# Token tile as the outer loop of the output projection and router, a slot list made on chip, and a gated down bias in one fp32r product

## What is computed

```python
h = h + memory_cross_attention(rmsnorm(h, norm_xa_g), mem, ...)   # ends in: o @ xa_wo
xt = rmsnorm(h, norm_ffn_g).reshape(n, d)
logits = xt @ router_w + router_b
top_val, top_idx = lax.top_k(logits, 4)
gates = softmax(top_val)
# tokens sorted by expert; slot_tok[slot] = token of that slot
gu = xt[tok] @ w_gu[e] + b_gu[e]
g, u = minimum(gu[:, :F], 7.0), clip(gu[:, F:], -7.0, 7.0)
y = ((u + 1.0) * (g * sigmoid(1.702 * g))) @ w_down[e] + b_down[e]
h = h + scatter_add(y * gates)
```

## Time and profile before

| | |
|---|---|
| median of 3 runs | 2607.06 us (2603.6 to 2607.36) |
| the profiled execution | 2609.65 us, of which the span from first to last instruction is 2608.0 us |
| PE busy | 2352.2 us (90%) |
| DVE busy | 1590.6 us (61%) |
| ACT busy | 1117.3 us (43%) |
| POOL busy | 350.5 us (13%) |
| mean granted clock of PE | 0.93 of full speed |

### The profile page before, as it was taken

How to read it: one execution, slowest core, us unless ns; L and a number is a source line. 1 busy time by engine, 2 the same in 40 slices (tenths; PEclk the granted TensorE clock), 3 DMA queues, 4 the chain that set the end, 5 groups by cost and what they waited for, 6 DMA issues and landing times.

```text
span 2608.0 us, 31503 instructions
## 1 busy us (share of the span) xinstructions
PE 2352.2 (90%) x9494; PEld 1711.6 (66%) x9495; DVE 1590.6 (61%) x1522; ACT 1117.3 (43%) x1047; POOL 350.5 (13%) x338
## 2 busy tenths in 40 slices
PE   7997499989999956999999999999999999999960
PEld 4553374554554525888888888888888787778840
DVE  4446841110131366786876666787778779978748
ACT  4123120030130213565654544556566567765632
POOL 0370300000000052010110100111011011110016
PEclk9989659989999957999999999999999999999985
DMA  4002010130100116786876866778789789997857
GB/s 151 33 1 83 1 81 33 35 126 29 36 19 1 67 66 235 289 302 222 327 268 225 290 224 211 281 278 324 254 313 369 247 313 370 371 338 267 313 209 289
DMA packets 215265, 514.21 MB, mean 197 GB/s; under 512 B 19140, under 2 KB 19338, under 8 KB 214520
## 3 DMA queue, kind: packets, MB, share of 16 engines
q1 hardware_dynamic: 194912, 450.72, 48.5%
q0 software_dynamic: 18352, 62.60, 6.4%
q10 hardware_dynamic: 1960, 0.35, 0.1%
HBM read 481.97 MB, written 30.48 MB: 196 GB/s over the span
## 4 chain that ended last, share of the span: by engine, by line
PE 44%; issue 5%; DVE 5%; DMA 5%; ACT 2%; POOL 1%; DVEq 1%; ACTq 0%; POOLq 0%; SPq 0%
PE PS L839 17%; PE PS L860 10%; PE PS L843 9%; PE PS L867 5%; DVE WL L1602 2%; DMA WA<-in_exp_w_down 2%; DMA WA<-in_exp_w_gu 2%; PE PS L892 1%; PE PS L831 1%; DVE H L1212 1%; PE PS L804 1%; POOL WA L1884 1%; ACT WH L1112 1%; ACT WH L1117 1%; DVE XEL L1598 0%
## 5 line engine op out<-in xcount | busy, mean ns | idle before, releaser
L1602 DVE TENSOR_TENSOR WL<-WA,WH 128x2048 fp32r<-128x2048 f32 x384 | 876.6, 2290 | 288.4 <-ACT WH L1133 117.8
L839 PE MATMUL PS<-WH,XEL 128*128 128x512 f32 x1344 | 361.1, 391 | 0.0
L839 PE MATMUL PS<-WH,XEH 128*128 128x512 f32 x1344 | 360.7, 390 | 0.0
L843 PE MATMUL PS<-WL,XEH 128*128 128x512 f32 x1344 | 347.6, 390 | 0.0
L1117 ACT CAST WH<-WA 128x2048 fp32r<-128x2048 f32 x128 | 243.9, 1908 | 201.8 <-PE PS L843 150.5
L1112 ACT CAST WH<-WA 128x2048 fp32r<-128x2048 f32 x128 | 244.5, 1910 | 190.4 <-PE PS L843 155.0
L1133 ACT CAST WH<-WA 128x2048 fp32r<-128x2048 f32 x124 | 236.5, 1909 | 199.3 <-PE PS L867 181.8
L839 PEld LDWEIGHTS PS<-WH,XEL 128*128 128x128 f32 x1344 | 253.2, 188 | 53.3
L843 PEld LDWEIGHTS PS<-WL,XEH 128*128 128x128 f32 x1344 | 253.2, 188 | 52.9
L839 PEld LDWEIGHTS PS<-WH,XEH 128*128 128x128 f32 x1344 | 253.1, 188 | 52.1
L538 PE MATMUL PS<-XT,WB 128*128 128x512 f32 x512 | 223.2, 597 | 1.1 <-issue 1.1
(11 more groups left out here) (249 smaller groups left out, 2373.4 us busy)
## 6 DMA issues: line engine op xcount, KB each, us to landing
WA<-in_exp_w_gu SPq DMA_DIRECT2D x256, 1024.0 KB, 6.4
WA<-in_exp_w_down SPq DMA_DIRECT2D x128, 1024.0 KB, 6.1
y_rows<-WA POOLq DMA_DIRECT2D x42, 512.0 KB, 6.7
WB<-in_xa_wkv SPq DMA_DIRECT2D x4, 2048.0 KB, 8.0
WB<-in_w_in SPq DMA_DIRECT2D x3, 2048.0 KB, 10.4
H<-in_x SPq DMA_DIRECT2D x4, 1024.0 KB, 5.9
WB<-in_w_out SPq DMA_DIRECT2D x2, 2048.0 KB, 7.8
WA<-in_x SPq DMA_DIRECT2D x1, 4096.0 KB, 12.2
```

The source lines that it names most:

```text
L839: nc.tensor.matmul(PS[:, 2 * h + t, :], x[:, KT4 * half + k, t * P:(t + 1) * P], WH[:, j % 4, k * HALF:(k + 1) * HALF], start=False, stop= ...
L843: ins = nc.tensor.matmul(PS[:, 2 * h + t, :], XEH[:, KT4 * half + k, t * P:(t + 1) * P], WL[:, j % 4, k * HALF:(k + 1) * HALF], start=Fals ...
L1602: v.tensor_tensor(WL[:, s, :], RAW[:, s, :], WH[:, s, :].bitcast(F32), sub).then_inc(done, 1)
```

## The change

It has four pieces.

- **Tile outermost.** The units are ordered per tile: both halves of `wo2`, then `xt3` of the tile before, `rl` of the one before that and `rt` of the one before that. DVE makes the one-hot, `MS` and `CU` of each tile as its top 8 come in. The up bias's high and low parts move up to the first tiles.
- **Slot list on chip.** The scatter, the DRAM tensor and its reading back go. A slot number is split into row `PRW` and column `PCL`; for each of the 32 groups of 128 assignments DVE makes a one-hot of the column (`OHC`, 128x128) and a one-hot of the row times the token number (`OHR`, 128x98), and PE sums the 32 products `OHC^T OHR` in unit `idx`, which is the table itself.
- **Down bias.** `GF` is written three times side by side (`GF3`), so that its transpose has 96 rows: high, low, high. `BDN` is loaded three times; its copy is high, high, low. One fp32r matmul per unit then takes the place of one float32 matmul.
- **Order behind it.** `idx` and its copy come ahead of `gft`, the item table and `bd`; the first gather reads `IDX` directly and no longer waits for `ITM`. Behind `bd`, DVE makes the low part of the first weight block, then those of the tokens, then the other three blocks.

The diff, cut to its core:

```diff
-        order += [("wo2", c, l) for c in range(2) for l in range(L)]
-        for n in range(L + 2):
-            order += [("xt3", n, h) for h in range(2) if n < L]
-            order += [("rl", n - 1)] * (0 < n <= L) + [("rt", n - 2)] * (n >= 2)
-        order += [("rank",), ("cnt",), ("itm",), ("gft", 0), ("gft", 1)]
+        for n in range(L + 3):
+            order += [("wo2", c, n) for c in range(2) if n < L]
+            order += [("xt3", n - 1, h) for h in range(2) if 0 < n <= L]
+            order += [("rl", n - 2)] * (2 <= n < L + 2) + [("rt", n - 3)] * (n >= 3)
+        order += [("cnt",), ("rank",), ("idx",), ("gft", 0), ("gft", 1), ("itm",)]
         order += [("bd", l, c) for l in range(L) for c in range(2)]
-        order += [("idx",)]
...
             for j in range(4):
+                wait_filled(sp, ("xt3", 2 * j + 1, 1))
+                sp.wait_ge(xn_out[j], 32)
                 load_gate_up(j, slice(0, 1))
             sp.wait_ge(itm_done, 1)
-            sp.wait_ge(scat, 16 * TOPK * L)
-            sp.dma_start(TBI[0:NROW, :], slot_tok.rearrange("(r p) o -> r (p o)", p=P)).then_inc(tb_in, 16)
...
+            o = begin(("idx",))
+            for n in range(TOPK * L):
+                if n % (2 * L) == 0:
+                    pe.wait_ge(hot_done, n // (2 * L) + 1)
+                ins = mm(o[:, 0:NROW], OHC[:, n, :], OHR[:, n, :], n, TOPK * L)
+            end(("idx",), ins)
...
-                    end(("bd", l, c), mm(o, GTT[0:E, l * P:(l + 1) * P], BDN[0:E, c * HALF:(c + 1) * HALF], 0, 1))
-            pe.wait_ge(tbf_done, 1)
-            o = begin(("idx",))
-            end(("idx",), nc.tensor.transpose(o[:, 0:NROW], TBF[0:NROW, :], ident[0:NROW, 0:NROW]))
+                    end(("bd", l, c), mm(o, GT3[:, l * P:(l + 1) * P], BD3[:, c * HALF:(c + 1) * HALF], 0, 1))
...
                     d(v.max_index(TIu[:, l, :], TV[:, l, :], LG[:, l, :]))
+                    d(v.tensor_copy(TIf[:, l, :], TIu[:, l, :]))
+                    tt(OH4[:, :, l, :], TIf[:, l, 0:TOPK].unsqueeze(2).to_broadcast([P, TOPK, E]),
+                       IO.unsqueeze(1).to_broadcast([P, TOPK, E]), ALU.is_equal)
+                    d(v.tensor_reduce(MS[:, l, :], OH4[:, :, l, :].rearrange("p j e -> p e j"), AX.X, add))
+                    tt(CU[:, l + 1, :], CU[:, l, :], MS[:, l, :], add, s=ms_done if l == L - 1 else dve_step)
...
-            d(v.tensor_copy(POS, POSf), pos_done)
+            ts(PRW, POSf, 1.0 / P, 0.5 / P - 0.5, mul, add)
+            ts(PRW, PRW, 1.5 * 2 ** 23, None, add)
+            ts(PRW, PRW, 1.5 * 2 ** 23, None, sub)
+            stt(PCL, PRW, -float(P), POSf, mul, add)
+            for h in range(2):
+                n0 = 2 * L * h
+                v.tensor_tensor(OHC[:, n0:n0 + 2 * L, :], PCL[:, n0:n0 + 2 * L].unsqueeze(2).to_broadcast([P, 2 * L, P]),
+                                IOF[:, :].unsqueeze(1).to_broadcast([P, 2 * L, P]), ALU.is_equal)
+                for n in range(n0, n0 + 2 * L):
+                    ins = v.tensor_scalar(OHR[:, n, :], IOF[:, 0:NROW], PRW[:, n:n + 1], TOKF[:, n % L:n % L + 1],
+                                          ALU.is_equal, mul)
+                ins.then_inc(hot_done, 1)
...
+            tt(GF3.rearrange("p l (r e) -> p l r e", r=3), GF.unsqueeze(2).to_broadcast([P, L, 3, E]),
+               MTM.unsqueeze(2).to_broadcast([P, L, 3, E]), add, s=gf_done)
+            dve.wait_ge(bd_high, 1)
+            v.tensor_tensor(BD3[2 * E:3 * E, :], BDN[2 * E:3 * E, :], BD3[2 * E:3 * E, :].bitcast(F32), sub) \
+                .then_inc(bd3_done, 1)
+            wait_filled(dve, ("idx",))
+            evac(dve, v.tensor_copy(IDX[:, 0:NROW], bank(("idx",))[:, 0:NROW]), ("idx",), own=True)
...
+                dve.wait_ge(gt_high, h + 1)
+                evac(dve, v.tensor_tensor(low, bank(u)[E:2 * E, :], low.bitcast(F32), sub), u)
...
             for j in range(4):
                 dve.wait_ge(gu_high, j + 1)
                 low_weights(j, gu_low)
+                if j == 0:
+                    for half in range(2):
+                        dve.wait_ge(xeh_done, half + 1)
+                        low_tokens(half, 2)
...
-            for j in range(TOPK):
-                for l in range(L):
-                    g.indirect_dma_start(out=slot_tok[:, :],
...
-            g.tensor_copy(IDC, IDX[:, 0:2]).then_inc(idc_done, 1)
```

More of the change, by code:

```diff
@@ L176, in build @@
         POSf = YTf[:, 1152:1152 + 32]
-        POS = YTf[:, 1184:1216].bitcast(I32)
         ITE = YTf[:, 1224:1227]
@@ L773, in _ @@
             end(("itm",), mm(o[0:1, 2 * P:3 * P], ITE[:, 2:3], ident[:], 0, 1))
-            pe.wait_ge(gf_done, 1)
-            for h in range(2):
-                o = begin(("gft", h))
-                for j in range(4):
-                    ins = nc.tensor.transpose(o[0:E, j * P:(j + 1) * P], GF[:, 4 * h + j, :], ident[:])
-                end(("gft", h), ins)
-            pe.wait_ge(bdn_in, 16)
+            pe.wait_ge(bd3_done, 1)
             units_read(pe, "gft")
```

169 lines of the change are left out of this document (87 added, 82 removed).

## The result

| | kernel before | changed kernel |
|---|---|---|
| median of the runs, us | 2607.21 (2603.6 to 2608.28, 4 runs) | 2581.53 (2578.14 to 2584.7, 4 runs) |
| profiled execution, its span, us | 2609.65, 2608.0 | 2580.11, 2578.5 |
| granted clock, mean | 0.930 | 0.937 |
| first `wo2` matmul, us | 775.88 | 774.83 |
| first matmul of the item loop, us | 997.62 | 969.78 |

The ratio is 0.9904, with a 95% interval of 0.9887 to 0.9921: 25.7 us faster by the medians. The forecast was 2587, 20.2 us faster than the 2607.21 of these runs, in a range from 2578 to 2595.

What follows compares the result with a forecast made beforehand. It took the wait chain between router and first gate product, with scatters and gather ending last, as the bound. Banks free at 971.5 instead of 991.4 gave 19.9 us less: 2587 us, range 2578 to 2595.

Steps and rivals of the forecast that it cites:

- the rival of a full clock: Index product runs at full clock, DVE sets its end: 6 to 7 us earlier, 2581 us; chance 0.18.
- Router under the output product: Router work hides between output product tiles; last running sum done at 915.0 instead of 922.0, 7.0 us gained.
- the rival of a router that isn't hidden: A unit holds PE up in each tile, last sum stays near 922: 7 us lost, 2594 us; chance 0.04.
- the slower one: Clock falls to 1.2 GHz in the cut-up output product; kernel slower than before, up to about 2713 us; chance 0.02.
- Slot numbers: After the last running sum, counts come ahead of ranks on PE; slot numbers at 920.4, 2.1 us more gained.
- One-hots: DVE's 98-column operations with two scalars take 0.25 us each; each half 6.2 us, done at 927.5 and 933.7.
- The rival of 0.45 us: DVE's scalar operations for the one-hots cost 0.45 us each; index ends 3.6 us later, 2591 us; chance 0.13.
- The index product: 32 float32 matmuls, 64 records of 0.275 us at half clock; PE sets the end, 17.6 us, at 945.1.
- the list of signs: Marks to show the forecast right or wrong, among them 64 index records of some 0.27 us; half that length means wrong.
- Behind the index: Gates' transposes and low parts, slot arithmetic, item table and 16 additions: 26.4 us, banks free at 971.5 against 991.4.
- Start of the loop and the first item: Token transposes, copies and low parts take 6.2 us again; late refills taken at nothing, at most 4 us.
- the first item starves: Late refills reach ACT late and PE waits 3 to 4 us in the first item: 2590 to 2591 us; chance 0.10.

Runs made afterwards that it cites:

- the mixed run: Changed kernel with one more product, of rows 0 to 63 only, behind each of the 32 index products: 2617.61 us in a single execution.
- the run with the late start: Changed kernel with TensorE beginning the index products only when both halves of the one-hots are there: 2591.12 us in a single execution.
- the version whose loop starts 7 us earlier still: Changed kernel with tokens ahead of most down bias products, second slot arithmetic after low weights, earlier register loads, twelve additions before the first weight block: 2577.6 us, 0.9887.

## Why the prediction was right, and where it was not

It was right in its path and in its steps but one, and 5.5 us off in size. That one step, the index product, had both its price and the engine that ends it wrong. The time of 2581.5 us lies in the range, but where the rival of a full clock had put it (2581), not at the forecast's 2587. The marks, with the forecast's moved by the 1.05 us by which this run was early:

| mark | forecast | measured |
|---|---|---|
| end of the last `wo2` | 901.05 | 901.18 |
| last running sum | 913.95 | 914.19 |
| slot numbers complete | 919.35 | 919.95 |
| one-hots, first and second half | 926.45, 932.65 | 927.00, 933.05 |
| end of the index product | 944.05 | 937.24 |
| index list copied from | 944.35 | 938.64 |
| gates' transposes and low parts done | 947.35 | 940.34 |
| banks free | 970.45 | 963.77 |
| first matmul of the loop | 976.65 | 969.78 |

**Router under the output product.** Right to 0.3 us, against the rival of a router that isn't hidden and against the slower one: the window of 127.1 us is at 1.00, without a gap.

**Slot numbers.** Right to 0.4 us: 0.57 us of wait for the counts where 2.53 stood before.

**One-hots.** The forecast of 0.25 us for an operation of 98 columns with two scalars per partition was made between 0.16 and 0.446; it is 3.93 / 16 = 0.245. The rival of 0.45 us falls.

**The index product: the step that failed.** "For 98 columns I take 0.275, so 0.55 per matmul" and, from it, "so PE sets the end". The records cost 0.213 us at the half clock, 0.43 per matmul, between the lower bound of 0.33 and the forecast; 0.112 at the upper level is under that bound, which was made for the lower one. And TensorE was ready before DVE wanted the list. The row it was priced by held records of 64 and 128 rows in turn, which the forecast called "full 128-row weights"; with such a turn alone, as the mixed run shows, 0.213 becomes 0.34. The text read the mean of a window and didn't look at its single records. A better row was at hand: the prediction itself priced 8 transposes at 0.23 each from the 16 token transposes, which are of one height, at the same clock. With 0.23 the index product would have ended 2.9 us earlier. Scaling by columns was wrong too: those transposes have 128 columns and start 0.213 us apart, as the records of 98 do.

The rival "at the full clock" had 0.18. Its condition came true in part: the clock rose at 933 us, and the last 36 steps took 0.112 us, less than half of the 0.27 that the list of signs named. Its outcome came true in full: DVE sets the end, the loop starts 6.9 us earlier than forecast (the rival said 6 to 7). What the clock brought can be estimated. At 0.213 us to the end, the 64 records from 927.14 would have taken 13.9 us (0.30, 62 steps of 0.213, and 0.42 for the last record) and ended at 941.1, and the list is copied 0.04 us behind that, as in the run with the late start. DVE came for it at 938.64. So with the right price alone PE would still have set the end: of the 5.7 us by which the copy came early, 3.2 are the record's and **2.5 the clock's**. The forecast's sum had no place for a rise on the way; it took the lower level to the end.

The Trainium skill, "TensorE: Matmul & The Clock Gate", section "LDWEIGHTS (loading the stationary operand)", gives a load the time of its columns at 1.2 GHz, and the prediction added that to the columns to get 0.27 us. The trace disagrees with the sum: 0.213 us for a load and a product of one height together, and the mixed row's 0.34 is above it. The same page's section "Why this matters for your kernels" asks for a TensorE that is kept busy. The even index product agrees with it, 0.50 and then 1.00; the mixed one, without a gap for 43 us, stayed at 0.50.

**Behind the index.** The gates' transposes and low parts took 1.7 us behind the copy of the list instead of 3.0, since TensorE began them at the upper clock while DVE still had other work: 1.3 us. The second slot arithmetic and item table took 11.2 us for 11.4. Additions and banks took 12.2 us for 11.7. The bias products start 0.43 us apart, as estimated, until they have to wait for banks (from then on 0.72, the pace of the additions that free them); all of it lies under the additions. The gather, issued at 939.85 and 941.21, is waited for by nobody.

**Start of the loop and the first item.** 6.0 us for 6.2, and no gap of TensorE in the first item: the rival "the first item starves" falls for this kernel. In the version whose loop starts 7 us earlier still the first item did wait, but for VectorE's own work and not for refills that came late: ACT had the fifth block ready at 969.04 there, and VectorE took it at 974.88.

The deviations are -5.7 us (copy of the list), -1.3 (gates), -0.2, +0.5 and -0.2: together -6.9, and 19.9 + 6.9 are the 26.8 of the stretch. By the medians the gain is 25.7.

## What to carry to other kernels

A price taken from a window's mean is good only if the single records in it are of the kind that will run; look at their shapes, heights too, before scaling by columns. For the price of a record take the distance of starts; a window's count also holds the records that only reach into it. An edit under a longer wait is worth nothing alone and can be worth 12 us when that wait goes, so test parts both alone in the kernel before and taken out of the changed one. When several things end together at the head of a loop, count the engine's own way into the loop (here 4 to 5 us behind its last product) as one of them.

## What the runs showed of the hardware that was not expected

- Float32 records of 128 rows, with 98 columns as with 128, start 0.213 us apart at the half clock and 0.11 at the full one. A change between 64 and 128 rows costs another 0.25 to 0.30 us at the half clock (0.34 us a record when they take turns by two), and the clock stayed there for 43 us without a gap.
- TensorE's way into the nested item loop takes 5.0 and 4.8 us behind its last product, 4.1 with the two register loads done ahead; VectorE had 2.33 us there.
- Additions of 512 columns from PSUM that don't wait for their own end follow at 0.60 us (2.48 for four, in the kernels with four banks for the bias), with that wait at 0.72 (11.57 for 16).
